# Values turned inside the search stage, and first operands of attention set there

## What is computed

```python
for i in range(S // Q_BLOCK):                 # 16 blocks of 128 queries
    # group A: differential attention, 4 heads with two softmax maps each
    attn = softmax(s1) - lam * softmax(s2)
    o = einsum('bhqk,bkhv->bqhv', attn, v)    # v = av: 4 heads x 128 columns
    # group B: score every admissible key with 16 indexer heads, keep 256
    rel = relu(einsum('bqhd,bkd->bqhk', q_idx, k_idx))
    score = einsum('bqh,bqhk->bqk', w_idx, rel)
    top_val, top_idx = top_k(score, 256)
    # 8 query heads share one key/value head (bk, bv) over the kept keys
    p = softmax(logits + alibi, over top_idx)
x = x + g1 * (mix @ w_out);  x = x + g2 * mlp(x);  return rmsnorm(x)
```

## Time and profile before

| | us |
|---|---|
| median of the runs | 3327.0 |
| the profiled execution, its own time | 3334.68 |
| its span, first to last instruction | 3332.9 |
| what lies around the span | 1.8 |
| PE busy over the span | 3149.0 (94%) |
| DVE busy | 2443.4 (73%) |
| ACT busy | 1849.3 (55%) |
| POOL busy | 425.6 (13%) |

### The profile page before, as it was taken

How to read it: one execution, slowest core, us unless ns; L and a number is a source line. 1 busy time by engine, 2 the same in 40 slices (tenths; PEclk the granted TensorE clock), 3 DMA queues, 4 the chain that set the end, 5 groups by cost and what they waited for, 6 DMA issues and landing times. The chain is left out here.

```text
span 3332.9 us, 44382 instructions
## 1 busy us (share of the span) xinstructions
PE 3149.0 (94%) x15808; PEld 2546.8 (76%) x15808; DVE 2443.4 (73%) x4320; ACT 1849.3 (55%) x3101; POOL 425.6 (13%) x690
## 2 busy tenths in 40 slices
PE   4999999999978999999999899999999999999998
PEld 4787878888746777777777687788778878888787
DVE  5544998889956687878776688788878775655676
ACT  4312889899758989898986333322432233222232
POOL 0010223112201100000000000122121110000321
PEclk9999999999978999999999999999999999999999
DMA  7475444323356432221112364544454455655555
GB/s 239 135 244 156 132 122 129 102 88 115 112 161 163 106 84 52 53 50 52 39 29 80 126 207 137 191 151 149 148 164 159 160 199 209 244 197 179 196 204 199
DMA packets 330634, 471.73 MB, mean 142 GB/s; under 512 B 25328, under 2 KB 217024, under 8 KB 330032
## 3 DMA queue, kind: packets, MB, share of 16 engines
q1 hardware_dynamic: 280576, 305.09, 30.6%
q0 software_dynamic: 49840, 163.83, 14.5%
HBM read 311.84 MB, written 156.98 MB: 141 GB/s over the span
## 5 line engine op out<-in xcount | busy, mean ns | idle before, releaser
L2437 PE MATMUL m_ps<-m_h,w_hi 128*128 128x512 f32 x1792 | 558.4, 393 | 19.6 <-DVE w_lo L2039 10.3
L2437 PEld LDWEIGHTS m_ps<-m_h,w_hi 128*128 128x128 f32 x1792 | 337.6, 189 | 95.9 <-DVE w_lo L2039 16.3
L2450 PE MATMUL m_ps<-w_hi,a_hi 128*128 128x512 f32 x896 | 350.2, 391 | 6.3 <-DVE w_lo L2268 3.4
L1097 DVE SCALAR_TENSOR_TENSOR rank<-spare,iw,rank 128x1024 f32<-128x1024 f32 (+5 forms) x330 | 330.0, 1021 | 33.7 <-ACT spare L1010 29.6
L2437 PE MATMUL m_ps<-m_h,w_lo 128*128 128x512 f32 x896 | 351.0, 392 | 0.0
L2450 PE MATMUL m_ps<-w_lo,a_hi 128*128 128x512 f32 x896 | 349.9, 390 | 0.0
L2450 PE MATMUL m_ps<-w_hi,a_lo 128*128 128x512 f32 x896 | 349.7, 390 | 0.0
L1010 ACT ACTIVATE spare<-isps 128x1024 f32<-128x1024 f32 (+5 forms) x352 | 279.2, 825 | 58.7 <-PE isps L980 29.1
L980 PE MATMUL isps<-ki,iq 128*128 128x512 f32 (+3 forms) x1216 | 292.3, 373 | 11.0 <-ACT spare L1010 6.2
L980 PEld LDWEIGHTS isps<-ki,iq 128*128 128x128 f32 x1216 | 222.3, 189 | 77.2 <-ACT spare L1010 15.4
L3020 ACT ACTIVATE pt<-tps 128x512 f32<-128x512 f32 (+1 forms) x432 | 232.2, 584 | 54.8 <-PE ops L2972 26.7
(11 more groups left out here) (302 smaller groups left out, 6598.5 us busy)
## 6 DMA issues: line engine op xcount, KB each, us to landing
w_raw<-in_w_ff SPq DMA_DIRECT2D x136, 512.0 KB, 5.5
dram_aop<-a_out POOLq DMA_DIRECT2D x224, 256.0 KB, 2.6
a_lo<-dram_aop SPq DMA_DIRECT2D x56, 1024.0 KB, 5.8
queries<-dram_proj SPq DMA_DIRECT2D x128, 256.0 KB, 4.4
iq<-dram_proj SPq DMA_DIRECT2D x224, 128.0 KB, 3.0
ada_w<-in_w_ada POOLq DMA_DIRECT2D x16, 1024.0 KB, 6.4
dram_proj<-r_ev_hi POOLq DMA_DIRECT2D x104, 128.0 KB, 2.6
dram_proj<-r_ev_lo POOLq DMA_DIRECT2D x104, 128.0 KB, 2.8
```

Source lines behind the costliest of these rows:

```text
L1097: nc.vector.scalar_tensor_tensor(out=dst, in0=got, scalar=w, in1=dst, op0=ALU.mult, op1=ALU.add).then_inc(s_acc, 1)
L2437: mm = nc.tensor.matmul(ps[:, b], w[:, w1_slot(n, j), k, :], hop[:, j, h, :, k, :], start=fresh and k == 0 and i == 0, stop=k == KH - 1 an ...
L2450: mm = nc.tensor.matmul(ps[:, t], a[:, c % RING, k, t * P:(t + 1) * P], w[:, c % RING, k, :], start=first and i == 0, stop=last and i == 2 ...
```

## The change

`values` is taken out. Its work becomes jobs of the search stage's planner: `vload` (POOL issues the loads once all 68 rest units are multiplied and their stores have landed), `vturn` (PE, 16 turns for group A and 2 that hold all of group B) and `vcopy` (ACT copies all 18 out; DVE copies none). The tiles lie where `ht_hi` and `ht_lo` were, which nobody reads after the last rest unit. A job `ahead` on POOL, after the loads of the values, loads two query units, the shared key's first piece and six of eight key rows of group A's first piece, and makes the table of places: two iotas and two copies to floats, on POOL instead of DVE.

At the stage's end POOL no longer waits until the last `rank` row has landed in DRAM; it waits for that at the start of attention, ahead of clearing semaphores. In attention SP loads only the two key rows left of the first piece and queries from the third unit on. DVE trims the table with one minimum and one memset ahead of the first score, and the powers are made just before the first search. All planner constants of the search stage have new values, and `rank` buffers lie elsewhere.

```diff
-INDEX_SLACK = 0.0776
-REST_FROM, REST_PACE, ROUNDS, INDEX_MASK = 55.48, 0.304, -94.116, 2.53
-INDEX_PLACES = dict(index=-192.28, relu=-476.24, add=-11.58, chain0=-46.97, chain1=-70.11, keep=-249.63, split=222.78,
-                    lo=252.07, mm=-180.81, evac=98.46, evac_lo=-62.27, store=-310.36, kept_mask=-374.33,
-                    weights=-286.23)
+INDEX_SLACK = 0.0347
+REST_FROM, REST_PACE, ROUNDS, INDEX_MASK = 75.86, 12.486, -34.794, 169.04
+INDEX_PLACES = dict(index=-17.19, relu=-566.8, add=26.95, chain0=-84.64, chain1=-82.32, keep=-267.36, split=258.6,
+                    lo=110.56, mm=-14.26, evac=-14.83, evac_lo=-191.95, store=-481.49, kept_mask=-573.36,
+                    weights=-212.32, vload=20.2, ahead=-14.8, vturn=-70.63, vcopy=31.74)
...
+class Early:
+
...
+        self.va = sb("va", [P, NB, 512])
+        self.vb = sb("vb", [P, NB, DH])
+        self.kb = sb("kb", [P, SEQ], F32R)
+        self.table = sb("table", [P, SEQ])
+        self.second = sb("second", [P, SEQ])
+        self.queries = sb("queries", [P, QU, 4, 2, P], F32R)
+        self.diagonal = sb("diagonal", [P, GT])
+        self.low = sb("low", [P, GT])
+        self.ka = sb("ka", [P, 2 * A_HEADS, SEQ], F32R)
...
+    loads, copies = [], []
+    for n, (count, late) in enumerate(((2, 6.0), (2, 11.0), (1, 14.0), (1, 17.0), (3, 21.0))):
+        loads.append(put("vload", Step("vload", "Q", 0.55 * count, late, REST_FROM + REST_PACE * (len(REST_TILES) + n),
+                                       [(stores[-2], 0.0), (stores[-1], 0.0)], n=n)))
+    put("ahead", Step("ahead", "Q", 13.0, 9.0, REST_FROM + REST_PACE * (len(REST_TILES) + 6), [(loads[-1], -21.0)]))
+    for n in range(NB + 2):
+        after = [(loads[n // 4], 0.0), (copies[n - 4] if n >= 4 else ends[len(REST_TILES) * NG - 4 + n], 0.0)]
+        where = REST_FROM + REST_PACE * (len(REST_TILES) + n / NG)
+        turn = put("vturn", Step("vturn", "PE", 0.55 if n < NB else 1.26, 0.163, where, after, n=n))
+        copies.append(put("vcopy", Step("vcopy", "ACT", 0.48, 0.12, where, [(turn, 0.0)], n=n)))
...
+                def load_values(n):
+                    if n == 0:
+                        pool.wait_ge(s_mm, len(evacs))
+                        for m in range(2):
+                            pool.wait_ge(s_st[m], 16 * stored[m])
+                    if n < NG:
+                        pool.dma_start(early.ka[:, n, GT:].bitcast(F32).rearrange("p (c t) -> p c t", t=GT),
+                                       scr.av[0:3 * P, n * GT:(n + 1) * GT].rearrange("(c p) t -> p c t", p=P)
+                                       ).then_inc(s_vin[n], 16)
+                    if n == 0:
+                        pool.dma_start(early.low[:], scr.av[3 * P:, 0:GT]).then_inc(s_vin[0], 16)
+                    elif n == 1:
+                        pool.dma_start(early.kb[:, GT:].bitcast(F32), scr.av[3 * P:, GT:]).then_inc(s_vin[1], 16)
...
+                def load_ahead():
+
+                    for n in range(EARLY_UNITS):
+                        row = early_units[n] // DH
+                        view = scr.proj[row:row + 4, :, :, 0:P].rearrange("m r p q -> p (m r) q")
+                        for half in range(2):
+                            pool.dma_start(early.queries[half * DH:(half + 1) * DH, n].rearrange("p m r q -> p (m r) q")
+                                           .bitcast(F32), view).then_inc(s_ahead, 16)
+                    pool.dma_start(early.kb[:, 0:GT].bitcast(F32),
+                                   scr.proj[R_BK // DH, :, :, 0:GT].rearrange("r p t -> (r p) t")).then_inc(s_ahead, 16)
+                    for hm in range(EARLY_KEYS):
+                        pool.dma_start(early.ka[:, hm, 0:GT].bitcast(F32),
+                                       scr.proj[R_AK // DH + hm, :, :, 0:GT].rearrange("r p t -> (r p) t")
+                                       ).then_inc(s_ahead, 16)
+
+                def places():
+
+                    nc.gpsimd.iota(early.second[:].bitcast(I32), pattern=[[1, SEQ]], base=P - SEQ - (P - 1),
+                                   channel_multiplier=0).then_inc(s_place, 1)
+                    nc.gpsimd.iota(early.diagonal[:, 0:P].bitcast(I32), pattern=[[-1, P]], base=-(P - 1),
+                                   channel_multiplier=2).then_inc(s_place, 1)
+                    pool.wait_ge(s_place, 2)
+                    nc.gpsimd.tensor_copy(early.table[:], early.second[:].bitcast(I32)).then_inc(s_place, 1)
+                    nc.gpsimd.tensor_copy(early.diagonal[:, P:2 * P],
+                                          early.diagonal[:, 0:P].bitcast(I32)).then_inc(s_place, 1)
...
-                    pool.wait_ge(s_kept[n], 16 * kept[n])
+                    if n != (NB - 3) % 3:
+                        pool.wait_ge(s_kept[n], 16 * kept[n])
+                pool.wait_ge(s_ahead, 16 * (1 + EARLY_KEYS + 2 * EARLY_UNITS))
+                pool.wait_ge(s_place, 4)
+                early.rank_kept, early.ranks_kept = s_kept[(NB - 3) % 3], kept[(NB - 3) % 3]
...
+                    elif job.kind == "vturn":
+                        n = job.n
+                        if n < 4:
+                            pe.wait_ge(s_elo, streams["mm"][(len(evacs) - 4 + n) * KT + KT - 1].of.n_lo)
+                        else:
+                            pe.wait_ge(s_vout, n - 3)
+                        if n < NB:
...
+                        else:
+                            if n == NB:
+                                pe.wait_ge(s_idr, 1)
+                                pe.wait_ge(s_vin[NG], 48)
+                            for m in range(8):
+                                kt = 8 * (n - NB) + m
+                                for part in range(2):
...
+                                    mm = nc.tensor.matmul(ps[:, n % 4, m * DH:(m + 1) * DH], rows, ident_r[:],
+                                                          start=part == 0, stop=part == 1, skip_group_check=True)
+                        mm.then_inc(s_vt, 1)
...
+                    elif job.kind == "vcopy":
+                        act.wait_ge(s_vt, job.n + 1)
+                        if job.n < NB:
+                            to = early.va[:, job.n, :]
+                        else:
+                            to = early.vb[:, 8 * (job.n - NB):8 * (job.n - NB) + 8, :].rearrange("p n d -> p (n d)")
+                        nc.scalar.activation(to, ps[:, job.n % 4, :], ACT.Copy).then_inc(s_vout, 1)
...
-def values(nc, keep, scr, late, block, va, vb):
...
-            load_unit(0)
-            for dst, row in places:
+            for dst, row in places[EARLY_KEYS:2 * A_HEADS]:
                 load_keys(dst, row, 0)
-            load_chosen(2)
 
             pieces = [(dst, row, g) for g in range(1, NG) for dst, row in places]
             for n in range(1, len(units)):
-                load_unit(n)
+                if n >= EARLY_UNITS:
+                    load_unit(n)
+                if n == EARLY_UNITS:
+                    load_chosen(2)
...
+            pool.wait_ge(early.rank_kept, 16 * early.ranks_kept)
             pool.dma_reset(spent)
             pool.sem_clear(spent)
-            nc.gpsimd.iota(second[:].bitcast(I32), pattern=[[1, SEQ]], base=P - SEQ - (P - 1),
-                           channel_multiplier=0).then_inc(s_io, 1)
-
-            nc.gpsimd.iota(probs[:, 0, 0:P].bitcast(I32), pattern=[[-1, P]], base=-(P - 1),
-                           channel_multiplier=2).then_inc(s_io, 1)
+            nc.gpsimd.memset(bias[:, 0:1], 0.0).then_inc(s_free, 1)
...
-            pe.wait_ge(s_id, 2)
-            pe.wait_ge(s_va, NB)
-            pe.wait_ge(s_vb, NB)
+            pe.wait_ge(s_id, 3)
             seen = -1
-            groups = 0
+            groups = 1
+            early_keys = True
             for job in plan:
                 if job.kind == "score":
                     unit = job.n_unit
                     if unit > seen:
                         seen = unit
-                        pe.wait_ge(s_q[unit % QU], 32 * (unit // QU + 1))
+                        loads = unit // QU + (0 if unit % QU < EARLY_UNITS else 1)
+                        if loads:
+                            pe.wait_ge(s_q[unit % QU], 32 * loads)
+                    if early_keys and job.what != "sparse" and 2 * job.head + 1 >= EARLY_KEYS:
+                        early_keys = False
+                        pe.wait_ge(s_k[0], 16 * (2 * A_HEADS - EARLY_KEYS))
...
-            dve.wait_ge(s_io, 2)
-            then(nc.vector.tensor_copy(table[:], second[:].bitcast(I32)))
-            then(nc.vector.tensor_copy(probs[:, 1, 0:P], probs[:, 0, 0:P].bitcast(I32)))
-            then(nc.vector.tensor_tensor(table[:, SEQ - P:SEQ], table[:, SEQ - P:SEQ], probs[:, 1, 0:P], ALU.min))
-
-            then(nc.vector.memset(table[0:DH, SEQ - DH:SEQ], -BIG))
-            then(nc.vector.memset(powers[:, 0:1], -1.0))
-            at = 1
-            while at < TOPK_ROUNDS:
-                more = min(at, TOPK_ROUNDS - at)
```

(16 more changed lines are left out.)

141 lines of the change are left out of this document (67 added, 74 removed).

## The result

The changed kernel took 3308.3 us (median of 3299.8 to 3312.1), the kernel before beside it 3327.8 us (3326.3 to 3331.3). The ratio is 0.993, with an interval of 0.9919 to 0.9942: faster by 19.5 us where 28.8 were forecast. The prediction names two ranges: 3308.3 us lies inside the wider (3283 to 3313) and 0.3 us above the narrower (3288 to 3308). The profiled execution is 3311.0 us, against 3334.7 before: 23.6 us less.

A forecast was written before the change was run, and what follows sets the result against it. Search bound by PE until 900 us, then DVE, then a 40 us hole bound by no engine; 39.2 - 2.5 - 5.2 - 0 - 2.7 - 0 + 0 = 28.8 us saved, 3327.0 to 3298.2 us; range 3288 to 3308, wider 3283 to 3313.

The forecast's parts named there:

- new order of the stage: Search stage: new planner constants reorder every engine; taken as 0, bounded by 6 us either way, a tenth of DVE's idle time.
- copies and turns beside the adds: Search's last 45 us: 18 ACT copies delay DVE's adds by 2.7 to 7.7 us, taken as 5.2; PE's turns 0.
- POOL's cast: Search's end: POOL's copy of the table holds DVE for its whole length, taken as 2.7 us.
- powers: Attention's start: the powers, 1.0 us, are not removed but moved ahead of the first search on DVE's queue.
- Parts 1 and 2: Search's end and the hole behind it: earlier stage end, loads, turns and copies gone; first read 40.2 us earlier, gate 39.2.
- Part 3: Attention's start: waits for `rank_in`, third query unit and two key rows, no longer hidden; bounds 0 and 6 us, taken 2.5.
- Part 4: Search's last 45 us: moved work costs 5.2 us for copies, 0 for turns, 2.7 for POOL's copy, 0 for new order.
- rival a: Search's end: values come too late, rest units end after 923 us; 3310 us at an end near 935; chance 0.09.
- Part 5: Attention's first blocks: PE's clock falls as before, taken as 0; if it held, say 8 us saved.
- (b): Search's end: last rest unit at 960 us, behind the search, 37 us exposed; slower, 3335 us; chance 0.04.
- (c): Attention's first blocks wait for transfers, two or three waits of 4 to 6 us in a row; 3310 us; chance 0.07.
- (d): Search and attention's start: new order takes 6 us more from DVE's idle time, clock holds for some; 3285 us; chance 0.08.

The follow-up runs named there:

- e3: Kernel before with only the search stage's new planner constants (new order), nothing else of the change: 3323.1 us, ratio 0.9971 to the kernel before.
- e5: Changed kernel with the last six `iq` units in rows of their own, loaded ahead of POOL's burst: 3298.7 us, ratio 0.9904 to the kernel before.
- e10: e9 with the planner told that the first four groups of values land later, so turns stand later on PE: 3294.8 us, 0.9893 of the kernel before.
- e7: e5 with POOL's cast of the table of places made four times in a row instead of once: 3302.4 us, ratio 0.9914 to the kernel before.
- e11: e10 with keys that put turns and copies ahead of scores and relus: 3303.5 us, ratio 0.9919 to the kernel before.
- e9: e5 plus third query unit first in SP's queue and all eight key rows loaded ahead by POOL: 3296.6 us, ratio 0.9903 to the kernel before.
- e4: Changed kernel with the old planner constants for the jobs both kernels have: 3318.1 us, ratio 0.9957 to the kernel before.

## Why the prediction held, point by point

The forecast held in sign and in its wider range, but as a sum of errors, and that is luck in part: the last add, forecast at 957 to 965 us, came at 957.4 by an order that brought some 8 us and a starving that cost some 11, neither of them in the sum. Each part in turn, on the profiled pair:

| step | predicted | measured | read from |
|---|---|---|---|
| new order of the stage | 0 (6 either way) | 7.8 saved (8.9 in e3) | start of the 30 adds; e3 |
| copies and turns beside the adds | 5.2 lost | 1 to 1.5 lost | e5, e10 |
| POOL's cast | 2.7 lost | 0 here; 1.4 to 1.5 in e5, e7, e10 | in a gap of DVE |
| burst against SP's loads of `iq` | not priced | 11 to 11.5 lost | 12.5 of growth less the copies |
| last add to first read | 42.96 to 2.7 | 42.96 to 5.4 | 957.39, 962.77 |
| cold operands | 2.5 lost (0 to 6) | 6.4 lost | 13.3 - 5.9 - 1.0 |
| powers | 1.0 lost | 1.0 lost | |
| from the first search to the end | 0 | 2.0 lost | 25.6 less 23.6 |
| sum | 28.8 saved | 23.6 saved | |

**Parts 1 and 2, the hole, were right in kind.** Loads and most turns and copies left it. The step "all of loads, turns and copies leave it" was 2.7 us too generous: six copies and the turns of group B follow the last relu. The last of them ends 3.6 us behind the last add in the changed kernel and 4.7 in e10, and the first score stands 4.5 us behind the last add, where 2.5 at most were named as the sign. With the copies out of the way (e11) the first read came 2.4 us behind the last add, close to the 2.7 that were forecast.

**Part 3, cold operands, was under-sized.** The term was 2.5 us, the trace has 6.4, just past the bound. Its wait for the third unit was put at 1.2 us, from a median landing of 6.0 us. SP issued that unit 0.7 us behind the first score (962.67 us), even sooner than assumed, but PE could use it only at 973.98, some 11 us later: at a DMA share of 0.99 from 960 to 980 us the median no longer held. Taking medians for transfers at the start of a stage, where all of them start together, was the error. `rank_in`, which carried the upper bound, landed 8.5 us after its issue at 963.18 and was not waited for in the changed kernel, as the queries came later still. It did show once queries and keys were there (e9, 1.5 us; e11, 5.6 us).

**Part 4, the failed step is the one that isn't there.** The text moved 5 MB of loads and attention's first loads into the last 45 us of the search. It used their length only to ask whether they would be in time (rival a). It never asked what else is in the DMA engines then. The prices stood in the rows: at the 256 GB/s of the hole, where the DMA share was 0.78, the burst takes 20 us for the values alone and 30 with the rest, and `iq` has three buffers, reloaded only when a unit is multiplied. Queue by queue the text named SP and POOL as issuers, and not that both feed the same engines. e5 shows the cause: the same burst without those reloads beside it leaves 42.3 us for the 30 adds instead of 49.4 to 50.9, and 2.75 of the 42.3 are another wait for the burst, at the first turn.

**Copies, turns and the cast were over-sized, 7.9 us instead of 2.6 in e10.** The copies' price took the idle time of ACT per relu and charged the rest of each copy to DVE: 0.15 to 0.43 us each, the middle, for all 18. Two steps failed. Only 10 to 12 of the 18 stand between relus, the others follow the last one. And between relus it is the lower price that holds: where each relu is followed by a copy, the relus of e10 start 1.38 to 1.40 us apart (926.45, 927.85, 929.23) instead of 1.22, and the adds lose at most 0.1 to 0.14 a copy. e11 shows a price of some 0.4 where the copies are bunched. The 0 for the turns held in e10, but not where the first waits for its load (2.6 us in e5) or where the long ones of group B stand ahead of a score (e11).

The cast was placed rightly: one add was longer. In the changed kernel it fell into a gap and cost nothing. The way of reckoning was right, DVE is held while POOL reads; the size was off, as the cast's own length is 1.89 us (e10) and not 2.7, near the iota's 1.83, and an add is held for 1.4 to 1.6 of it. The 2.7 to 3.0 us of a cast in e5 and e7 are longer because POOL waits for the add under way. The Trainium skill's page "SBUF — State Buffer", section "Who interferes with whom", says that a DVE instruction with two SBUF inputs contends with a GpSimd instruction that reads SBUF. The trace agrees: 1.49 us for each cast in e7. That the price is the cast's whole length, as the prediction read that rule, comes near for a cast that needn't wait (1.53 of 1.89 us in e10), and not for one that does (1.43 of 2.97 in e5).

**The new order** was put at nothing, with a bound of 6 us "a tenth of the idle time". It brought 8.9 in e3, and 8.4 by the times (0.9971, clear of 1). e4 agrees in sign from the other side. No trace of before could have told this; the bound was too narrow, and it was a guess.

**Part 5, the clock, was right.** It stands at 0.51 from 960 to 980 us, at the lower of its two levels, as before. What it didn't see is that the clock fell for a while inside the search too, behind PE's waits for `iq` (0.86 from 925 to 950 us).

**The sums.** That part 4's bounds move the forecast "from 3291 to 3314" doesn't come out of them: taken singly they give 3292 to 3307 us, all together 3289 to 3317.

**The rivals.** (a) and (b) didn't come: the last rest matmul ended at 905.9 us, far ahead of 923. (c), attention's first loads late, came in part: one wait of 6.2 us, just past the 6 us that were named as its sign. The late `iq` is the same mechanism, a stage earlier than I had looked for it. Of (d) the half on the order came, the half on the clock didn't.

**What stays open.** The 2 us between first search and end, as the other profiles scatter by as much (2328.7 to 2333.8 us). How much of the 11 us is PE's slow clock behind its waits and how much the waits themselves (8.0 us). Why the block's start scatters by 5 us from one profile to the next. That the shares of the two queues go by packets: the count of 1596 to 1367 speaks for it, and so does the rule in the Trainium skill's page "DMA: Bandwidth & Descriptors", section "Queues, rings and completion order", that a DMA engine takes turns between its queues packet by packet. No run changed the size of `iq`'s packets. By such a rule larger packets on SP's side, or smaller ones on POOL's, would be the cure; that wasn't tried.

## What to carry to other kernels

When loads are moved to where they are hidden, ask whose loads are already there: a DMA share near 1 for 20 us did no harm to the burst, but made small loads that a full pipeline waits for with three buffers up to 18 us late. Give such loads room to be issued ahead of the burst. Moved work on an engine with a little idle time per step was nearly free one piece at a time, and cost some three times as much in bunches, so place it by the times at which the traces show its operands to land. And when a hole is closed, list the transfers that it had been hiding in the order in which they will be missed; moving one forward only uncovers the next.

## What the runs showed of the hardware

- **Two queues on full DMA engines share by packets, it seems, not by bytes.** From 920 to 945 us the profile has 1596 packets and 6.14 MB on POOL's queue against 1367 and 0.66 MB on SP's. Loads of 128 KB that land after 2.9 us at the median took up to 20.7 to 23.1 us.
- **DVE and a full DMA can run beside each other.** In e10, DVE was busy for 97% of 40.5 us, at a DMA share of 0.99 and 287 GB/s, and the median add took 1283 ns, as the 1284 of e3 at a share of 0.24.
- **A POOL cast and a two-input add of DVE take turns.** A cast of 128x2048 from int32 to f32 lasts 1.89 us when it begins just ahead of an add (e10) and 2.97 when it begins just behind one (e5). It holds one add for 1.4 to 1.5 us either way (adds of 2809 and 2710 ns instead of 1284). A cast of 128x128 lasts 0.29 us with DVE idle (changed kernel) and 1.29 beside an add (e10).
- **PE's clock fell inside the search** when its loads starved: 0.86 from 925 to 950 us in the changed kernel, where PE was busy for 17.04 of 25 us, and 1.00 in e10, where it was busy for 37.97 of 40.5.
